# Two transformer blocks, 256 tokens: mLSTM head scaling folded into the gate, a reordered first norm and a finer last store

## The reference, cut to what matters

```python
def rmsnorm(x, g):
    return x * lax.rsqrt(jnp.mean(x * x, axis=-1, keepdims=True) + EPS) * g
...
def ab_mixer(h, w_in, b_i, b_f, head_gain, w_out):
    mq, mk, mv, mo, mi, mf, sq, sk, sv = _split(h @ w_in, AB_SIZES)
    hm = mlstm(...)                    # 4 heads of 128: h = num / max(|den|, exp(-m_t))
    hm = rmsnorm(hm, head_gain) * sigmoid(mo)
    hs = stick_breaking(...)           # 4 heads of 128
    return concatenate([hm, hs]) @ w_out
```

## Time and profile before

| what | value |
|---|---|
| median of three runs | 1313.63 us (1311.4 to 1314.0) |
| profiled execution, its own time | 1312.71 us |
| its span | 1311.0 us |
| TensorE busy | 1266.3 us, 97% |
| VectorE busy | 792.0 us |
| ScalarE busy | 707.2 us |
| mean granted clock of TensorE | 0.992 |

### The profile page before, as it was taken

The page is one execution under the profiler, slowest core; times in us unless marked ns, Lnnn a source line. Parts: engine busy times, 40 slices in busy tenths (PEclk is TensorE's granted clock), DMA queues, the critical chain, the costliest instruction groups (busy, mean ns, idle before and its releaser), DMA issues.

```text
span 1311.0 us, 22040 instructions
## 1 busy us (share of the span) xinstructions
PE 1266.3 (97%) x9160; PEld 1148.5 (88%) x9160; DVE 792.0 (60%) x1163; ACT 707.2 (54%) x1118; POOL 128.8 (10%) x146
## 2 busy tenths in 40 slices
PE   6999999999999988999999999999999999999997
PEld 6988899998889877898999888988998898999886
DVE  5776578885467565654555446777545645655443
ACT  5766666664467544645555335554355644655433
POOL 6000001110000000000211000104700000111000
PEclk9999999999999998999999999998999999999999
DMA  9433455555555524543655554533203544455550
GB/s 338 156 108 127 145 176 179 193 176 196 178 167 184 176 83 133 186 161 97 192 174 183 193 179 158 166 124 113 97 4 112 182 140 160 148 177 190 193 193 32
DMA packets 141430, 205.52 MB, mean 157 GB/s; under 512 B 3730, under 2 KB 118802, under 8 KB 141330
## 3 DMA queue, kind: packets, MB, share of 16 engines
q1 hardware_dynamic: 141330, 204.11, 47.2%
HBM read 203.05 MB, written 1.05 MB: 156 GB/s over the span
## 4 chain that ended last, share of the span: by engine, by line
PE 85%; DVE 7%; ACT 4%; issue 2%; POOL 1%; DMA 1%; SPq 0%; DVEq 0%; ACTq 0%
PE ps L303 41%; PE ps L365 27%; PE ps L383 6%; DVE weights_lo L282 2%; PE ps L2079 2%; PE ps L2141 1%; ACT weights_hi L279 1%; PE ps L1703 1%; PE ps L1725 1%; PE ps L487 1%; POOL arena L2367 1%; DVE split_arena L518 1%; ACT normed L904 1%; DMA weights<-in_w_in 1%; PE ps L755 0%
## 5 line engine op out<-in xcount | busy, mean ns | idle before, releaser
L282 DVE TENSOR_TENSOR weights_lo<-weights,weights_hi 128x1024 fp32r<-128x1024 f32 x379 | 471.0, 1254 | 254.0 <-ACT weights_hi L279 251.9
L303 PE MATMUL ps<-split_arena,weights_hi 128*128 128x256 f32 x3056 | 562.2, 286 | 8.0 <-DVE split_arena L518 6.4
L279 ACT ACTIVATE weights_hi<-weights 128x1024 fp32r<-128x1024 f32 x379 | 396.7, 1056 | 263.6 <-PE ps L365 182.7
L303 PEld LDWEIGHTS ps<-split_arena,weights_hi 128*128 128x128 f32 x3056 | 479.8, 193 | 16.5 <-issue 11.9
L303 PE MATMUL ps<-split_arena,weights_lo 128*128 128x256 f32 x1528 | 433.8, 284 | 0.0
L303 PEld LDWEIGHTS ps<-split_arena,weights_lo 128*128 128x128 f32 x1528 | 294.7, 193 | 0.0
L365 PE MATMUL ps<-weights_hi,split_arena 128*128 128x512 f32 x992 | 272.7, 392 | 2.4 <-ACTq L1876 1.6
L365 PEld LDWEIGHTS ps<-weights_hi,split_arena 128*128 128x128 f32 x992 | 184.5, 188 | 41.8 <-issue 2.9
L365 PE MATMUL ps<-weights_lo,split_arena 128*128 128x512 f32 x496 | 153.6, 390 | 0.0
L365 PEld LDWEIGHTS ps<-weights_lo,split_arena 128*128 128x128 f32 x496 | 93.1, 188 | 19.7
L1884 POOL TENSOR_TENSOR normed<-normed 128x512 f32<-128x512 f32 x32 | 34.1, 1065 | 491.8 <-ACTq L1876 491.8
(11 more groups left out here) (364 smaller groups left out, 1314.1 us busy)
## 6 DMA issues: line engine op xcount, KB each, us to landing
weights<-in_mlp_w SPq DMA_DIRECT2D x64, 1024.0 KB, 5.4
weights<-in_w_up SPq DMA_DIRECT2D x22, 1024.0 KB, 5.1
weights<-in_c_w_in SPq DMA_DIRECT2D x16, 1024.0 KB, 5.4
weights<-in_w_in SPq DMA_DIRECT2D x14, 1024.0 KB, 6.2
weights<-in_ab_w_in SPq DMA_DIRECT2D x12, 1024.0 KB, 5.4
weights<-in_w_down SPq DMA_DIRECT2D x11, 1024.0 KB, 5.0
weights<-in_xa_wv SPq DMA_DIRECT2D x8, 1024.0 KB, 5.0
weights<-in_xa_wq SPq DMA_DIRECT2D x8, 1024.0 KB, 5.2
```

Source lines behind the costliest of these rows:

```text
L279: act.activation(h, r, ACT.Copy).then_inc(s_hi, 1)
L282: dve.tensor_tensor(l, r, h.bitcast(F32), ALU.subtract).then_inc(s_lo, 1)
L303: mm = pe.matmul(o, w[:, k, :], x[:, k, :], start=(k == 0 and i == 0), stop=(k == DC - 1 and i == 2))
```

## The change

- **First norm.** `first_norm_act` and `first_norm_dve` take the place of `norm_act` and `norm_dve` for norm 0. ScalarE squares tile 0 alone; VectorE squares tile 1 with a fused multiply and sum, with the mean of tile 0's first half between its two squares.
- **First splits.** Both engines split part 0, turn two banks, split part 1, and turn the other two. The transfer of unit 0 is issued in two pieces of 128 columns; ScalarE's split of part 0 waits for the first piece alone.
- **mLSTM heads.** `finish` copies bank 6 whole, denominators too, into RAW, and signals; then it sums the raw squares with a fused instruction. `head_means` makes all eight denominators' reciprocals at once and scales the sums by them twice. `head_gates` makes one factor for each head and token (reciprocal root times reciprocal denominator), and multiplies raw head, factor and gate in one instruction for each head and tile, heads 0 and 1 at s = 8 and heads 2 and 3 at s = 9. The first turn waits for the first of these two steps only.
- **End.** Each tile is scaled and stored in two halves.

```diff
@@ weights_sp
+                if n == 0:
+                    sp.dma_start(dst[:, :, 0:P], src[:, :, 0:P]).then_inc(s_first_part, 16)
+                    dst, src = dst[:, :, P:256], src[:, :, P:256]
                 sp.dma_start(dst, src).then_inc(s_unit[slot], 16)
@@ split
-                    act.wait_ge(s_unit[n % RING], 16 * (n // RING + 1))
+                    if p == 0:
+                        act.wait_ge(s_first_part, 16)
+                    else:
+                        act.wait_ge(s_unit[n % RING], 16 * (n // RING + 1))
...
+        def first_norm_act():
+            act.wait_ge(s_x_in[0], 16)
+            for h in range(2):
+                act.activation(HN[:, 0, half(h)], X[:, 0, half(h)], ACT.Square,
+                               accum_out=stat[:, h:h + 1]).then_inc(s_stat, 1)
+            for t in range(TT):
+                if t == 0:
+                    act.wait_ge(s_stat, 2)
+                act.wait_ge(s_mean0, t + 1)
+                act_then(act.activation(lnv[:, t:t + 1], stat[:, 2 * t + 1:2 * t + 2], ACT.Ln,
+                                        bias=mean0[:, t:t + 1], scale=1.0 / D))
+                act.activation(rstd[:, t:t + 1], lnv[:, t:t + 1], ACT.Exp, scale=-0.5).then_inc(s_rstd, 1)
+                act.wait_ge(s_rstd, t + 1)
+                act.activation(HN[:, t, half(0)], X[:, t, half(0)], ACT.Copy,
+                               scale=rstd[:, t:t + 1]).then_inc(s_hn_act, 1)
+            act.sem_inc(s_stat, 2)
+
+        def first_norm_dve():
+            dve.wait_ge(s_x_in[1], 16)
+            for h in range(2):
+                x = X[:, 1, half(h)]
+                dve_then(dve.tensor_tensor_reduce(out=HN[:, 1, half(h)], in0=x, in1=x, scale=1.0, scalar=0.0,
+                                                  op0=ALU.mult, op1=ALU.add, accum_out=stat[:, 2 + h:3 + h]))
+                if h == 0:
+                    first_half_dve(0, 0)
+            dve.tensor_scalar(mean0[:, 1:2], stat[:, 2:3], 1.0 / D, EPS, ALU.mult, ALU.add).then_inc(s_mean0, 1)
+            dve.wait_ge(s_x_in[0], 16)
+            for t in range(TT):
+                dve.wait_ge(s_rstd, t + 1)
+                dve.tensor_scalar(HN[:, t, half(1)], X[:, t, half(1)], rstd[:, t:t + 1], None,
+                                  ALU.mult).then_inc(s_hn_dve, 1)
@@ ab_pe, turn
-                pe.wait_ge(named("ab_om"), 2)
+                pe.wait_ge(named("ab_om"), c // 2 + 1)
@@ ab_dve, finish
-                dve_then(dve.scalar_tensor_tensor(out=dn[:, 0, :], in0=o[:, :, 128], scalar=-1.0,
-                                                  in1=GC[:, :, 32 + n], op0=ALU.mult, op1=ALU.max))
-                dve_then(dve.tensor_tensor(dn[:, 0, :], o[:, :, 128], dn[:, 0, :], ALU.max))
-                dve_then(dve.reciprocal(dn[:, 1, :], dn[:, 0, :]))
+                dve.tensor_copy(RAW[:, n, :, :],
+                                PS[:, 6, 0:258].rearrange("p (t n) -> p t n", t=TT)).then_inc(named("ab_o"), 1)
+                dve.wait_ge(named("ab_o"), n + 1)
                 for t in range(TT):
-                    ins = dve.tensor_scalar(OM2[:, t, n * P:(n + 1) * P], o[:, t, 0:P], dn[:, 1, t:t + 1], None,
-                                            ALU.mult)
-                ins.then_inc(named("ab_o"), 1)
+                    h = RAW[:, n, t, 0:P]
+                    ins = dve.tensor_tensor_reduce(out=OM2[:, t, n * P:(n + 1) * P], in0=h, in1=h, scale=1.0, scalar=0.0,
+                                                   op0=ALU.mult, op1=ALU.add, accum_out=HST[:, 0, n, t:t + 1])
+                if n == 3:
+                    dve_then(ins)
+
+            def head_means():
+                den = RAW[:, :, :, 128]
+                dve_then(dve.scalar_tensor_tensor(out=DN[:, 0, :, :], in0=den, scalar=-1.0,
+                                                  in1=GC[:, :, 32:36].rearrange("p t n -> p n t"),
+                                                  op0=ALU.mult, op1=ALU.max))
+                dve_then(dve.tensor_tensor(DN[:, 0, :, :], den, DN[:, 0, :, :], ALU.max))
+                dve_then(dve.reciprocal(DN[:, 1, :, :], DN[:, 0, :, :]))
+                dve_then(dve.tensor_tensor(HST[:, 1, :, :], HST[:, 0, :, :], DN[:, 1, :, :], ALU.mult))
+                dve.tensor_tensor(HST[:, 2, :, :], HST[:, 1, :, :], DN[:, 1, :, :],
+                                  ALU.mult).then_inc(named("ab_ssq"), 1)
+
+            def head_gates(g):
+                if g == 0:
+                    dve.wait_ge(named("ab_hrs"), 1)
+                    dve_then(dve.tensor_tensor(DN[:, 0, :, :], HST[:, 4, :, :], DN[:, 1, :, :], ALU.mult))
+                    dve.wait_ge(named("gate_gain"), 2)
+                for n in (2 * g, 2 * g + 1):
+                    for t in range(TT):
+                        cols = slice(n * P, (n + 1) * P)
+                        ins = dve.scalar_tensor_tensor(out=OM2[:, t, cols], in0=RAW[:, n, t, 0:P],
+                                                       scalar=DN[:, 0, n, t:t + 1], in1=SGM[:, t, cols],
+                                                       op0=ALU.mult, op1=ALU.mult)
+                ins.then_inc(named("ab_om"), 1)
@@ final_dve
-                dve.scalar_tensor_tensor(out=HN[:, t, :], in0=X[:, t, :], scalar=rstd[:, t:t + 1],
-                                         in1=row[:, ROW_FINAL:ROW_FINAL + D], op0=ALU.mult,
-                                         op1=ALU.mult).then_inc(named("final"), 1)
+                for h in range(2):
+                    dve.scalar_tensor_tensor(out=HN[:, t, half(h)], in0=X[:, t, half(h)], scalar=rstd[:, t:t + 1],
+                                             in1=row[:, ROW_FINAL + 512 * h:ROW_FINAL + 512 * (h + 1)], op0=ALU.mult,
+                                             op1=ALU.mult).then_inc(named("final"), 1)
@@ final_sp
-                sp.dma_start(out[t * P:(t + 1) * P, :], HN[:, t, :]).then_inc(s_out, 16)
+                for h in range(2):
+                    sp.wait_ge(named("final"), 2 * t + h + 1)
+                    sp.dma_start(out[t * P:(t + 1) * P, half(h)], HN[:, t, half(h)]).then_inc(s_out, 16)
@@ engines' programs: first norm, then
-            split(act, 1)
+            split(act, 0)
             act.wait_ge(s_early, 16 * 2)
-            turn_act(0, HT, LN_MIX)
+            turn_act(0, HT, LN_MIX, lambda c2: split(act, 1) if c2 == 1 else None)
```

More of the change, by code:

```diff
@@ L189, in build_two_blocks @@
         s_unit = [sem(f"unit_landed_{i}") for i in range(RING)]
+        s_first_part = sem("first_part_landed")
         s_hi = sem("weights_hi_ready")
@@ L1271, in build_two_blocks @@
         W3 = view(73 * 256, (2, 384))
-        HSQ = view(65 * 256, (TT, 4, P))
-        HST = view(69 * 256, (4, 8))
+        RAW = view(65 * 256, (4, TT, 129))
+        HST = view(69 * 256 + 16, (5, 4, TT))
         GC = view(62 * 256, (TT, 36))
-        DN = view(63 * 256, (4, 2, 2))
+        DN = view(63 * 256, (2, 4, TT))
         SQK_TILE = (0, 4, 2, 6)
@@ L1477, in ab_act @@
                     act.wait_ge(named("ab_ssq"), 1)
-                    act_then(act.activation(HST[:, 1, :], HST[:, 0, :], ACT.Ln, bias=eps_c[:, 0:1], scale=1.0 / P))
-                    act.activation(HST[:, 2, :], HST[:, 1, :], ACT.Exp, scale=-0.5).then_inc(named("ab_hrs"), 1)
+                    act_then(act.activation(HST[:, 3, :, :], HST[:, 2, :, :], ACT.Ln, bias=eps_c[:, 0:1],
+                                            scale=1.0 / P))
+                    act.activation(HST[:, 4, :, :], HST[:, 3, :, :], ACT.Exp, scale=-0.5).then_inc(named("ab_hrs"), 1)
                 if s in AB_TURN_AT:
@@ L1593, in ab_dve @@
                 if s == AB_SSQ_AT:
-                    dve.wait_ge(named("ab_o"), 4)
-                    head_squares_dve(OM2, HSQ, HST, 4, "ab_ssq")
+                    head_means()
                 if s in AB_GATE_AT:
-                    dve.wait_ge(named("ab_hrs"), 1)
-                    dve.wait_ge(named("gate_gain"), 2)
-                    head_gate_dve(OM2, AB_GATE_AT[s], HST, 4, SGM, "ab_om")
+                    head_gates(AB_GATE_AT[s])
                 if s in AB_TURN_AT:
@@ L1603, in ab_dve @@
                     out_low(AB_WEIGH_AT[s])
-        def head_squares_dve(o_all, sq, st, heads, told):
-            for t in range(TT):
-                o = o_all[:, t, :].rearrange("p (h d) -> p h d", h=heads)
-                dve_then(dve.tensor_tensor(sq[:, t, :, :], o, o, ALU.mult))
-                dve_then(dve.tensor_reduce(st[:, 0, heads * t:heads * (t + 1)], sq[:, t, :, :], AX.X, ALU.add))
-            dve.sem_inc(named(told), 1)
-        def head_gate_dve(o_all, t, st, heads, gate, done):
-            o = o_all[:, t, :].rearrange("p (h d) -> p h d", h=heads)
-            r = st[:, 2, heads * t:heads * (t + 1)].unsqueeze(2).to_broadcast([P, heads, P])
-            dve_then(dve.tensor_tensor(o, o, r, ALU.mult))
-            dve.tensor_tensor(o, o, gate[:, t, :].rearrange("p (h d) -> p h d", h=heads),
```

(7 more changed lines are left out.)

7 lines of the change are left out of this document (2 added, 5 removed).

## The result

The changed kernel takes 1300.21 us (median of 4 runs, 1299.37 to 1300.42) against 1312.55 for the kernel before on the same chip (1311.4 to 1314.0): ratio 0.9904, 95% interval 0.9892 to 0.9917, faster by 12.3 us where 10.8 were forecast. The profiled execution took 1300.14 with a span of 1298.4, so 12.6 less than before's profiled one.

The account below looks back on a forecast made before the run. TensorE, busy 97% of the span, was taken as the bound, so only its pauses and lower clock pay. Start 1.4, mixer 8.8 and end 0.6 sum to 10.8, off 1313.63: 1302.8 us, range 1300.5 to 1306.8.

Parts of the forecast that it names:

- The start, 1.4: Kernel start: first product earlier through reordered splits, new first norm and halved transfer; gain 1.4 us, bounds 0.6 to 2.4.
- The clock: Start: first product at 1.2 GHz until about 18.65; lead 1.35 stays whole if the rise comes forward, else 0.76.
- The end, 0.6: Kernel end: last tile scaled and stored in halves, 0.65 less to move; gain 0.6 us, bounds 0.1 to 0.9.
- The mixer, 8.8: mLSTM (ab) mixer: shorter waits for head scaling, split and gates, and no clock fall; 8.8 us, bounds 5 to 9.3.
- The clock's 2.5: ab mixer: without the long pauses the granted clock does not fall to 0.50; worth 2.0 + 0.5 = 2.5 us.
- a clock of 0.50 in the ab mixer: Sign that would show the forecast wrong: granted clock of 0.50 anywhere in the ab mixer.
- The lead did not shrink between 500 and 530: Sign that would show the forecast wrong: the lead shrinking between 500 and 530 us.
- The squares: First norm: tile 1's two squares (2 x 0.62) leave ScalarE; second scaled copy starts at 8.4, not 8.75.
- The first transfer: Start: unit 0 in two pieces, first there near 8.2; shorter rows cost no rate; 0.5 lost if at 9.58.
- GpSimd in the way of the squares: Rival, start: GpSimd contention slows each VectorE square by 0.5; start gains only 0.4, time 1303.8; chance 0.10.
- Late gates: Rival, ab mixer: first gates end 2.5 later and the clock falls again; gain 5.8, time 1307.8; chance 0.08.
- The slow clock at the start: Rival, start: TensorE stays at 1.2 GHz, each us costing 0.44; slower if some 31 us more; chance 0.03.

Follow-up runs that it names:

- start_alone: Kernel before with only the change's start (first norm, order of splits, halved first transfer): 1310.38 us, ratio 0.9980.
- before_busy_start: Kernel before plus 22 unread filler products ahead of the first norm's transposes and 12 behind them: 1311.24 us, ratio 0.9989.
- act_squares: Changed kernel with the first norm's squares of both tiles back on ScalarE: 1302.05 us, ratio 0.9916 to the kernel before.
- heads_alone: Kernel before with only the change's mLSTM heads part (copy, squares behind it, gates): 1302.92 us, ratio 0.9925.
- mixer_busy_14: Kernel before plus 14 unread filler products in the 4.1 us pause before the mLSTM mixer's first gates: 1308.62 us, ratio 0.9967.
- both_gates: Changed kernel whose first turn waits for both pairs of heads' gates again: 1303.98 us, ratio 0.9936 to the kernel before.
- norm_busy_before: Kernel before with unread filler products in the pauses at 799, 801 and 804 us, around the delta mixer's norm: 1312.16 us, ratio 0.9991.
- after_again: The changed kernel measured again, unchanged: 1300.76 us, ratio 0.9908 to the kernel before.
- all_busy: Changed kernel with unread filler products at the start, around the delta mixer's norm and before two sets of its solve's blocks: 1298.41 us, ratio 0.9888.
- start_and_solve_busy: Changed kernel with unread filler products around the first transposes and before the delta mixer's first solve blocks: 1299.93 us, ratio 0.9896.

## Why the prediction was wrong, and by how much it was off

The way and the mechanism came as forecast, but two terms of the sum were too small and its base too high, and the time fell 0.3 below the range.

- **What bounds the kernel** held: nothing but pauses and clock of TensorE paid. The work taken from VectorE and ScalarE moved the time only there.
- **The start, 1.4**, was mis-sized: 2.2 in the trace. The step that failed is "The clock": I let the rise of the rate come forward at most with the start, and took the lead of 1.35 whole or at 0.76. The product began at 12.77, not 12.4 (the mean at the upper bound, 6.65, and the logarithm 0.25 behind it), but the low rate, which had lasted until 18.65, ended 2.4 us earlier in start_alone and 5.9 or more in the changed kernel's profile. The run before_busy_start shows 2.0 for the clock with no earlier product. The pause of 0.98, at which the full rate outruns the third turn, takes the rest back; so the early clock of the changed kernel's profile and the later one of act_squares end 0.1 apart. This was not one lucky trace: in the six profiles with the old start and no fillers in it, the full rate stayed for good only from 17.7 to 19.9 on; in the six with the new order of splits and no fillers there, from 16.3 at the latest. The sums of squares came at 24.4 to 25.8 in the first six and at 22.9 to 23.7 in the others. That the shorter pause before the first product (0.8 to 1.6 in place of 2.5 to 3.2) is the reason fits these profiles and before_busy_start, but wasn't tested by itself.
- **The end, 0.6**, was mis-sized: 1.3 in the trace, above its bound of 0.9. The store is issued 4.28 behind the last matmul in place of 4.0, 0.3 worse, but lands 2.1 after issue in place of 3.6. I took the half of the bytes at 0.65; the landing fell by 1.5. Part of this is the execution that I had: beside heads_alone and start_alone, whose whole last stores landed after 2.6, halving gives only 0.3 to 0.4.
- **The mixer, 8.8**, held in its size and nearly in its terms: 0.41 for the copy (0.42 taken), 1.0 for the means (0.95), no wait before the score product, 0.27 at the turn (0.1). The clock's 2.5 was measured alone (mixer_busy_14), and both_gates brought wait and half rate back. That "the pauses of 1.2 and 1.85 at 463 and 473 left it at 1.00" is true of the trace that I had; in three other profiles with the same pauses (start_alone, before_busy_start, norm_busy_before) 3.4 us of half rate followed the first of them.
- **The signs.** One sign of being wrong came true, a clock of 0.50 in the ab mixer: the stretch at 452. It cost 1.4 and was absent in after_again. The lead did not shrink between 500 and 530 (9.6 at both ends).
- **The squares** I left in the start's list as a help; in the traces they are worth nothing that can be told.
- **The first transfer.** Its first half landed 5.6 after issue, at 8.3, as forecast (8.2). My reason did not follow: 512 KB in 4.0 against 1024 KB in 5.1 is fewer bytes per us, so these rows don't show that short rows cost nothing. Unit 0's landing in the profile that I had (9.58) was at the early end: three profiles with a whole unit have 9.6 to 9.7 and five 10.2 to 10.3, and against 10.26 the halves save 0.74 in the trace.
- **The rivals.** GpSimd in the way of the squares: they met and the squares took 0.79 and 0.68, not 0.5 more. The Trainium skill (SBUF — State Buffer, Who interferes with whom) says a VectorE instruction with two SBUF inputs contends with a GpSimd instruction that reads SBUF, and that whoever has the ports blocks the other; the trace agrees, GpSimd's select from 6.03 took 0.72 and ended 0.15 behind the square. The scaled copy that I counted for that rule has one tensor from SBUF beside a value for each partition, so it is no case of two such inputs, though it did wait. Late gates did not come (both_gates is what they would cost). The slow clock at the start did not come.
- **The time.** 1302.8 - 1300.2 = 2.6: 1.1 is the base, three runs of before with a median of 1313.63, which one more run brought to 1312.55 beside the changed kernel, and 1.5 the gain. Of it 0.8 is the start and 0.7 the end, by the traces, which explains the 1.5; the stretches at 452 and 804 of the two profiled executions nearly cancel (0.3, the difference of 12.6 in the spans to 12.3 in the medians). The gain of 12.3 itself lies within the 12.6 of my upper bounds; it is the base that took the time out of the range. The range's low end had half a us for such spread, and single executions differ by 2.8 for the changed kernel and by 4.5 for before beside the last three runs.

What stays open: why a stretch comes behind one pause in this execution and behind another in that. With the pauses at 790, 896 and 903 filled, none came in all_busy, and all its executions granted 0.998 or more; a single profile proves less, since the stretch at 804 is absent in mixer_busy_14 and heads_alone with no filler near it. The one at 452 stands behind a pause of only 0.59, and the same pause has none behind it in after_again. The stretches are not the whole spread either: executions of the kernel before with the same mean clock, 0.992, took from 1310.97 to 1314.36. The landing of the last store, 2.6 or 3.6, may be a part of it.

## What to carry to other kernels

Where TensorE is busy 97% of the span, sum the pauses and the half-rate stretch behind each: the longest pause, 4.1, stood for 6.6 with the 2.5 of half rate behind it. Look at several executions before a term of 1 to 2 us is believed, the landing of the last store included, for stretches of 3.4 or 6.8 us at half rate move among the pauses. Ordering splits by when each is first asked for paid, and so did halving the last store, by 0.3 to 1.3; moving the squares to a free engine did not, since ScalarE then waited 1.19 for the mean and began the first split only 0.08 earlier.

## What the runs showed of the hardware

- Pauses of 0.6 to 4.1 us in a kernel that is otherwise busy are followed by 3.4, 6.8 or 10.2 us at half clock in some executions and by none in others; 3.4 us of it cost 1.4 and 1.7, the 6.8 us in the mixer 2.5. Behind the pauses that fillers cut to 0.2 to 0.4 (norm_busy_before, all_busy, start_and_solve_busy) none was seen. The Trainium skill (TensorE: Matmul & The Clock Gate, What's actually happening) says that the number of slow matmuls at a kernel's start varies from run to run of one kernel; the runs here agree, with the rate full at 12.77 in the changed kernel's profile and low until 16.3 in start_alone's, which has the same start.
- A store of 256 KB landed 2.0 to 2.1 after issue in every profile, one of 512 KB 2.6 to 3.6; the last of two such stores took 3.6 in five profiles and 2.6 in heads_alone and start_alone.
- VectorE's scaled copy of 128x512 took 1.07 (heads_alone) to 1.49 (the kernel before, act_squares) where GpSimd's memset of 102x1536 had begun before it, and ended 0.5 behind the memset's end in each; it took 0.48 when the memset came later.
